# Moving five low-part subtractions of each attention stage from VectorE to GpSimd, with a semaphore of their own

## What is computed

```python
def hybrid_layer(x, ...):
    h = rms_norm(x, g_attn_pre)
    proj = h @ w_in + b_in
    mq, mk, mv, sq, sk, sv = split(proj)
    mq, mk, sq, sk = (apply_rope(a, cos, sin) for a in (mq, mk, sq, sk))
    mo = rms_norm(moba_attention(mq, mk, mv), g_moba_out)
    so = rms_norm(swa_sink_attention(sq, sk, sv, sinks), g_swa_out)
    x = x + rms_norm(concatenate([mo, so]) @ w_out, g_attn_post)
    h = rms_norm(x, g_ffn_pre)
    f = silu(h @ w_gate) * (h @ w_up)
    return x + rms_norm(f @ w_down, g_ffn_post)
```

## Time and profile before

| | |
|---|---|
| median of three runs | 576.99 us (576.7 to 577.41) |
| the profiled execution | 576.57 us |
| its span in the trace | 574.8 us |
| PE busy | 566.5 us, 99% |
| PE weight loads | 467.0 us, 81% |
| DVE busy | 374.3 us, 65% |
| ACT busy | 293.9 us, 51% |
| POOL busy | 232.3 us, 40% |
| w_l subtractions on DVE (L793) | 90 of them, 206.1 us |
| granted TensorE clock | 1.00 nearly throughout (mean 0.998) |

### The profile page before, as it was taken

One profiled execution on the slowest core, in us unless ns is written; L12 is line 12 of the kernel. 1 busy time (PEld: TensorE's weight loads), 2 busy tenths in 40 slices (PEclk: granted clock), 3 DMA queues, 4 the chain that ended last, 5 costly groups with the idle time before them and its releaser, 6 DMA issues.

```text
span 574.8 us, 8319 instructions
## 1 busy us (share of the span) xinstructions
PE 566.5 (99%) x3107; PEld 467.0 (81%) x3107; DVE 374.3 (65%) x486; ACT 293.9 (51%) x420; POOL 232.3 (40%) x452
## 2 busy tenths in 40 slices
PE   8999999999999999999999999999999999999996
PEld 6777877888888889888888888778888888898884
DVE  6789875946745747265597987576846746645722
ACT  7575755664345354163546655674644354325420
POOL 1100001607797797800120000043297797799100
PEclk9999999999999999999999999999999999999999
DMA  8953642538555550478265443516565564352701
GB/s 304 389 205 123 237 148 109 222 114 315 202 211 196 175 215 29 193 285 303 91 238 200 158 164 131 201 47 247 218 258 192 174 217 178 119 220 81 286 1 74
DMA packets 18729, 107.32 MB, mean 187 GB/s; under 512 B 2816, under 2 KB 3072, under 8 KB 7168
## 3 DMA queue, kind: packets, MB, share of 16 engines
q1 hardware_dynamic: 18688, 106.78, 50.3%
HBM read 105.72 MB, written 1.05 MB: 186 GB/s over the span
## 4 chain that ended last, share of the span: by engine, by line
PE 88%; DVE 6%; DMA 3%; ACT 1%; issue 1%; DVEq 0%; POOLq 0%; SPq 0%; POOL 0%; ACTq 0%
PE bank L1177 81%; PE bank L1217 4%; DMA raw<-in_w_blocks 3%; PE bank L1269 2%; PE bank L1242 2%; DVE w_l L793 1%; DVE bank L902 1%; DVE work L855 1%; DVE work L877 1%; DVE work L878 1%; DVE work L943 0%; DVE w_l L807 0%; ACT w_h L543 0%; DVE work L883 0%; ACT work L592 0%
## 5 line engine op out<-in xcount | busy, mean ns | idle before, releaser
L793 DVE TENSOR_TENSOR w_l<-raw,w_h 128x2048 fp32r<-128x2048 f32 x90 | 206.1, 2298 | 115.5 <-ACT w_h L543 115.4
L1177 PE MATMUL bank<-w_h,actT_h 128*128 128x512 f32 (+1 forms) x600 | 230.3, 384 | 0.4 <-DVE work L855 0.3
L543 ACT ACTIVATE w_h<-raw 128x2048 fp32r<-128x2048 f32 x90 | 171.9, 1915 | 110.0 <-PE bank L1177 90.1
L1177 PE MATMUL bank<-w_h,actT_l 128*128 128x512 f32 (+1 forms) x600 | 225.6, 376 | 0.0
L1177 PE MATMUL bank<-w_l,actT_h 128*128 128x512 f32 (+1 forms) x600 | 225.2, 375 | 0.0
L501 POOL COPY work<-work 32x128 f32<-32x128 f32 (+1 forms) x384 | 191.6, 499 | 75.4 <-DVE work L983 59.6
L1177 PEld LDWEIGHTS bank<-w_h,actT_h 128*128 128x128 f32 x600 | 113.1, 188 | 23.6 <-issue 2.2
L1177 PEld LDWEIGHTS bank<-w_h,actT_l 128*128 128x128 f32 x600 | 112.9, 188 | 21.0
L1177 PEld LDWEIGHTS bank<-w_l,actT_h 128*128 128x128 f32 x600 | 113.1, 189 | 18.8
L488 POOL TENSOR_TENSOR norms<-norms,constants 128x1 f32<-128x1 f32 x8 | 1.5, 193 | 146.8 <-ACT bank L640 146.8
L1177 PE MATMUL bank<-w_h,fT_h 128*128 128x512 f32 x160 | 49.4, 390 | 0.0
(11 more groups left out here) (77 smaller groups left out, 403.1 us busy)
## 6 DMA issues: line engine op xcount, KB each, us to landing
raw<-in_w_blocks SPq DMA_DIRECT2D x90, 1024.0 KB, 4.8
bias<-in_b_in SPq DMA_DIRECT2D x8, 256.0 KB, 5.6
raw<-in_w_blocks SPq DMA_DIRECT2D x4, 256.0 KB, 5.2
raw<-in_w_blocks SPq DMA_DIRECT2D x2, 512.0 KB, 7.6
x<-in_x SPq DMA_DIRECT2D x2, 512.0 KB, 10.5
gain_b<-in_g_attn_post SPq DMA_DIRECT2D x2, 512.0 KB, 7.4
bias<-in_g_ffn_pre SPq DMA_DIRECT2D x2, 512.0 KB, 5.5
gain_b<-in_g_ffn_post SPq DMA_DIRECT2D x2, 512.0 KB, 5.8
```

The lines of the kernel that those rows point to most:

```text
L543: nc.scalar.activation(w["h"][:, slot(b), :], raw[:, r, :], ACT.Copy).then_inc(hi_ready, 1)
L793: nc.vector.tensor_tensor(w["l"][:, slot(b), :], raw[:, slot(b, RAW), :], w["h"][:, slot(b), :].bitcast(F32), ALU.subtract).then_inc(lo_re ...
L1177: ins = nc.tensor.matmul(bank[BANK_OF[name]][:, 0:n], left[s][:, at + k, tokens(t)], right[r][:, k, c * BANK:c * BANK + n], start=first an ...
```

## The change

A tuple `POOL_LOW` names blocks 5, 6, 7, 8 and 10. DVE's `lo` returns without an instruction for them; POOL has a `lo` of its own with the same subtraction, which signals `pool_lo_ready`. `low_done` gives, for a block, the semaphore that its low part raises and the count to wait for. PE (before the first tile) and SP (before a load into a `raw` place) wait through it.

```diff
+POOL_LOW = (5, 6, 7, 8, 10)
...
+        def low_done(L, b):
+
+            mine = [c for c in range(NB) if (c in POOL_LOW) == (b in POOL_LOW)]
+            return pool_lo_ready if b in POOL_LOW else lo_ready, L * len(mine) + mine.index(b) + 1
...
-                    place_free(lo_ready, L * NB + before(b, RAW) + 1)
+                    last = before(b, RAW)
+                    place_free(*low_done(L + last // NB, last % NB))
...
+            def lo(L, b):
+
+                pool.wait_ge(hi_ready, L * NB + b + 1)
+                nc.gpsimd.tensor_tensor(w["l"][:, slot(b), :], raw[:, slot(b, RAW), :],
+                                        w["h"][:, slot(b), :].bitcast(F32), ALU.subtract).then_inc(pool_lo_ready, 1)
+
...
             for L in range(depth):
+                lo(L, 5)
+                lo(L, 6)
+                lo(L, 7)
+                lo(L, 8)
                 rms_o(L, SWA, 0)
                 rms_o(L, SWA, 1)
+                lo(L, 10)
                 rms_o(L, MOBA, 0)
...
             def lo(L, b):
 
+                if b in POOL_LOW:
+                    return
                 dve.wait_ge(hi_ready, L * NB + b + 1)
...
                     if t == 0:
-                        pe.wait_ge(lo_ready, L * NB + b + 1)
+                        pe.wait_ge(*low_done(L, b))
```

More of the change, by code:

```diff
@@ L243, in trunk @@
         lo_ready = sem("lo_ready")
+        pool_lo_ready = sem("pool_lo_ready")
         block_used = sem("block_used")
```

## The result

The changed kernel takes 599.27 us (median of six runs, 597.38 to 600.19), against 577.42 (576.7 to 578.02) for the kernel before in the same comparison: a ratio of 1.0377 [1.0357, 1.0397] (brackets hold the 95% interval, here and below). The profiled execution took 598.77 us with a span of 597.0; before it was 576.57 with 574.8.

What follows compares the result with a forecast made beforehand. PE was taken as the bound, so freed DVE time counted nothing; holds of DVE by POOL cost 13.4 + 3.5 + 2 x 2.1 = 21.1 us, giving 576.57 + 21.1 = 597.7 us, with an 8 in 10 range of 583 to 607.

Steps and rivals of the forecast that it cites:

- The bound: Both attention stages: PE lacks only 1.14 of 200.00 us, so freeing DVE gains at most about 1 us.
- The hold, both ways: A POOL subtraction stops DVE's next instruction with two SBUF inputs until it ends, and the reverse; PSUM readers are exempt.
- T: Length of one POOL subtraction of 128x2048: taken as 4.6 us, from sixteen copies of 0.286 us.
- its other estimate, 3.7: POOL subtraction length with the copy slope doubled for two inputs; by the same walk 13 us lost, 589.6 us.
- Layer 0, rope: Column group 1's second tile, behind blocks 5 and 6: rope ends at 43.9, PE wanting it at 38.0, stalls 5.9 us.
- Layer 0, round 1 and 2: Blocks 5 to 8: maxima start at 52.5, not 43.23, and 67.2, not 53.75; layer 0 pays 13.4 us.
- The slower array: Inside a rival: PE matmuls run slower after a stall (0.37 us each against 0.23), 2.1 us more in layer 0.
- Block 10: Both layers: scaling of o (L932) waits 4.6 us, maxima come 2.35 late against 0.2 slack; 2.1 us per layer.
- Layer 1: Blocks 5 to 8: rope 1.7 us late, round 2's maxima 5.3 late against 1.8 slack; pays 3.5 us.
- DVE not held: Rival: DVE keeps its inputs and POOL alone waits; 575.5 to 578 us, likeliest 576.5; chance 0.13.
- the short hold: Rival: POOL subtraction near 1.94 us, round 2's maxima of layer 0 start 3.2 late, 579.8 us; chance 0.08.
- the long hold: Rival: POOL subtraction of 5.5 us or more, or slower PE behind the stalls; some 606 to 610 us; chance 0.11.

Runs made afterwards that it cites:

- tiny: The kernel before, nothing on POOL, with DVE subtracting only the first 64 of 2048 columns of blocks 5, 6, 7, 8 and 10: 576.5 us, 0.9991.
- pieces8: The changed kernel with each POOL subtraction cut into 8 pieces of 128x256, no waits between them: 586.33 us, 1.016 to the kernel before.
- memsets: The changed kernel with POOL filling w_l with zeros in three linked pieces, reading nothing, instead of subtracting: 576.29 us, 0.999 to the kernel before.
- copies: The changed kernel with POOL copying raw to w_l, one input instead of two, in place of the subtraction: 579.71 us, 1.005 to the kernel before.
- filled: The changed kernel with 44 and 24 extra PE transposes inside layer 0's two longest waits to keep the clock up: 597.7 us, 1.036 to the kernel before.
- only10: The changed kernel with only block 10 on POOL, the other four blocks back on DVE: 581.28 us, 1.0069 to the kernel before.
- only78: The changed kernel with only blocks 7 and 8 on POOL, the other three back on DVE: 589.58 us, 1.0217 to the kernel before.
- chunks: The changed kernel with each POOL subtraction cut into 16 pieces of 128x128, no waits between them: 594.0 us, 1.0287 to the kernel before.
- linked16: The changed kernel with each POOL subtraction in 16 pieces of 128x128, each waiting on a semaphore from the one before: 602.74 us, 1.0423 to the kernel before.
- only12: The changed kernel with only block 12 on POOL, behind rms_o of MoBA's first tile, the five blocks back on DVE: 577.29 us, 1.0005 to the kernel before.

## Why the prediction was right

The forecast, 597.7 us, is 1.6 below the median of 599.27 and well inside the range. Point by point:

- **The bound.** "PE can take back at most about 1 us" of what DVE is freed: tiny shows 0.5 us (0 to 1.0 by its interval [0.9982, 1.0001]).
- **The hold, both ways.** Taken from a 2.48 us step on POOL and 0.1 us on DVE. In the changed profile L898 takes 4.30, L941 2.91 and L953 5.08 us, each to within a microsecond of POOL's end. Seen held are L877, L878 (5.05 us in layer 1, 0.68 before), L909, L920 and L932, the other rope steps only by pieces (pieces8); L793 met no hold in any of the rows read. Seen exempt are L902 and L855. That reads on POOL matter is shown by memsets against copies; the exemption of readers of PSUM is read from the traces only.
- **T.** Taken as 4.6, measured 4.51 to 4.60 (median 4598 ns, up to 5.01 where it also waits for DVE). That the estimate from sixteen copies came out is luck: nothing in the working ties a two-input subtraction to sixteen whole copies, and its other estimate, 3.7, gave 589.6 us, almost 10 short. The copy measures 1.90, the predicted low end, so the second input and the arithmetic cost 2.7. The Trainium skill's figure (GPSIMD Engine Reference, Elementwise — side-by-side cycle accounting), 4497 ns, agrees within 0.1 us.
- **Layer 0, rope.** Predicted end 43.9 and a stall of 5.9; measured 44.08 (0.6 of it start-up) and 5.38.
- **Layer 0, round 1 and 2.** Maxima predicted at 52.5 and 67.2, 13.4 late; measured 53.22 and 67.49, 13.1 late without the start-up's 0.6.
- **Layer 0, what was missed.** From there to the first MoBA maxima another 0.9 us went: the half clock behind the 3.04 us wait. The sum had no term for it. The slower array stood among the rivals only, at 2.1 us for the first stall. It did come behind both stalls, but filled gets only about 0.3 us back behind the first and 1.0 behind the second.
- **Block 10.** Predicted 2.1 a layer; the second MoBA maxima are 2.1 later than the first were. only10 gives 3.9 for both layers.
- **Layer 1.** Predicted 3.5 + 2.1 = 5.6, measured 5.5. Round 2's maxima were forecast 5.3 late and are 4.9 (354.66 against 333.05 and the 16.70 carried in). The two waits of PE forecast there at 2 us are 1.36 and 1.13.

In sum 15.5 predicted and 16.1 measured in layer 0, 5.6 and 5.5 in layer 1, plus 0.6 of start-up. Of the rivals, DVE not held falls by L898's 4.30; the short hold needed another T, and copies shows that it then goes as written; of the long hold only its clock part came, about 1.3 us against its 2.1, and mostly behind the other wait.

Some expectations of the runs did worse than the prediction: only78 by the clock behind a wait of PE, chunks by a rule carried from one instruction to sixteen, linked16 by what a link adds to each piece (0.585 us in place of 0.46), which I had priced too low.

## What to carry to other kernels

Before moving an elementwise operation to GpSimd to relieve VectorE, ask first whether VectorE sets the end (cut the work to a sliver and time it: here 0.1%), then list what VectorE has due during it that reads two SBUF tensors. Each such meeting costs up to the whole GpSimd instruction, shows as a long VectorE instruction, and costs time only if TensorE is waiting behind it; a place with no such reader due (only12) costs nothing. Cutting the instruction into pieces shortens the hold, but brings overhead a piece, and with pieces that stand ready one behind the other a VectorE instruction can be passed by many of them.

## What the runs showed that was not expected

- **A VectorE instruction can be passed many times.** With 64 GpSimd subtractions of some 0.46 us standing without a gap for 29.24 us, a product of 0.69 us took 13.08: 30 pieces that started no earlier than it went first. With 8 pieces of 0.74 a block the longest was 2.11, passed by two pieces and let in when GpSimd had none left; with a semaphore between pieces the longest were 1.2 and 0.97. So it takes more than GpSimd instructions ready one behind the other, since most products that met such pieces waited for one at most, in layer 1 of chunks too; a link between pieces fits its absence, from one profile each. The times of all four executions of chunks, 593.17 to 595.0, lie 7 us above those of pieces8, which fits its recurring. What picks the victim is open.
- **A fill holds nobody.** 13.94 us of GpSimd fills, which only write, cost the two-input VectorE instructions under them nothing, where a copy of 1.90 held one for 1.89.
- **TensorE's clock** fell to 0.50 behind a wait of 5.38 us and again behind one of 3.04, and was at 1.00 again from about 49 and 73, 5 and 3 us after the waits ended; waits of up to 1.5 us in layer 1 left it at 1.00. The length of the last wait doesn't decide alone: in only78 it fell behind one of 1.81, in pieces8 it stood at 1.00 behind one of 2.20. What such a fall cost depended on what lay ahead of it: 0.3 us where a hold covered it, 1.0 where none did.
